# Transposes between units, and a gate projection in four parts among the levels of a two-block transformer kernel

## What is computed

```python
o_a = gated_delta_rule_chunked(q_a, k_a, v_a, beta, log_decay)   # then norm and gate z
o_b = native_sparse_attention(q_n, k_cmp, v_cmp, k_slc, v_slc, k_win, v_win, gates, ...)
merged = (sigmoid(merge_a) * (o_a @ w_branch_gdn) + sigmoid(merge_b) * (o_b @ w_branch_nsa))
x = x + merged @ w_out
gate, up = split(rms_norm(x, ffn_norm_gain) @ w_gate_up, 2)
x = x + (silu(gate) * up) @ w_down                               # then a last rms_norm
```

## Time and profile before

| | |
|---|---|
| Median of 3 runs | 912.6 us (912.44 to 913.03) |
| Profiled execution | 912.57 us, its span 910.8 us |
| Granted TensorE clock, mean | 0.997 |
| Busy: PE, DVE, ACT, POOL | 888.0, 567.8, 437.8, 52.8 us |
| DMA | 151.71 MB, mean 167 GB/s |

### The profile page before, as it was taken

One profiled execution on the slowest core, in us unless ns is written; L12 is line 12 of the kernel. 1 busy time (PEld: TensorE's weight loads), 2 busy tenths in 40 slices (PEclk: granted clock), 3 DMA queues, 4 the chain that ended last, 5 costly groups with the idle time before them and its releaser, 6 DMA issues.

```text
span 910.8 us, 14487 instructions
## 1 busy us (share of the span) xinstructions
PE 888.0 (97%) x5984; PEld 776.8 (85%) x5984; DVE 567.8 (62%) x856; ACT 437.8 (48%) x632; POOL 52.8 (6%) x79
## 2 busy tenths in 40 slices
PE   7999999999999999999999999999999999999997
PEld 5999999899999888888779999677877788888885
DVE  4955564573657665655569878754376677777544
ACT  6744444744344544444356514753434455555441
POOL 1000000000030110000020141000000000000000
PEclk9999999999999999999999999999999999999999
DMA  9657744455455545555667665004664565655441
GB/s 297 222 185 216 225 140 138 139 185 184 125 156 184 184 145 180 164 195 188 215 188 160 166 138 188 1 3 139 139 231 151 171 188 188 187 186 193 170 162 46
DMA packets 127799, 151.71 MB, mean 167 GB/s; under 512 B 16967, under 2 KB 93126, under 8 KB 127734
## 3 DMA queue, kind: packets, MB, share of 16 engines
q1 hardware_dynamic: 127594, 150.70, 53.3%
q0 software_dynamic: 64, 0.07, 0.0%
q10 hardware_dynamic: 76, 0.02, 0.0%
HBM read 148.67 MB, written 3.68 MB: 167 GB/s over the span
## 4 chain that ended last, share of the span: by engine, by line
PE 88%; DVE 6%; ACT 2%; DMA 1%; issue 1%; SPq 1%; POOL 0%; POOLq 0%; DVEq 0%; ACTq 0%
PE bank L511 21%; PE bank L513 20%; PE bank L512 20%; PE bank L1217 9%; PE bank L1205 5%; DVE w_lo L1907 2%; DVE arena L2268 1%; DMA arena<-in_mem 1%; PE bank L790 1%; PE bank L915 1%; PE bank L691 1%; PE bank L671 1%; PE bank L1029 1%; PE bank L1010 1%; ACT w_hi L1393 1%
## 5 line engine op out<-in xcount | busy, mean ns | idle before, releaser
L1907 DVE TENSOR_TENSOR w_lo<-ring,w_hi 128x2048 fp32r<-128x2048 f32 (+1 forms) x134 | 301.0, 2251 | 176.3 <-ACT w_hi L1393 175.8
L1393 ACT ACTIVATE w_hi<-ring 128x2048 fp32r<-128x2048 f32 (+1 forms) x134 | 250.2, 1870 | 124.0 <-PE bank L513 83.4
L511 PE MATMUL bank<-h_both,w_hi 128*128 128x256 f32 x624 | 179.3, 287 | 1.7 <-DVE w_lo L1907 1.7
L512 PE MATMUL bank<-h_both,w_hi 128*128 128x256 f32 x624 | 176.5, 283 | 0.0
L513 PE MATMUL bank<-h_both,w_lo 128*128 128x256 f32 x624 | 176.5, 283 | 0.0
L1217 PE MATMUL bank<-h_both,w_hi 128*128 128x512 f32 x352 | 123.4, 398 | 0.0
L511 PEld LDWEIGHTS bank<-h_both,w_hi 128*128 128x128 f32 x624 | 119.6, 192 | 3.8 <-DVE w_lo L1907 2.3
L512 PEld LDWEIGHTS bank<-h_both,w_hi 128*128 128x128 f32 x624 | 119.7, 192 | 0.6 <-issue 0.5
L513 PEld LDWEIGHTS bank<-h_both,w_lo 128*128 128x128 f32 x624 | 119.7, 192 | 0.0
L1205 PE MATMUL bank<-h_both,w_lo 128*128 128x256 f32 x352 | 97.8, 281 | 0.4 <-ACT h_both L1416 0.4
L1408 ACT ACTIVATE arena<-bank 128x512 f32<-128x512 f32 (+5 forms) x91 | 45.5, 522 | 100.3 <-PE bank L513 87.3
(11 more groups left out here) (332 smaller groups left out, 1362.4 us busy)
## 6 DMA issues: line engine op xcount, KB each, us to landing
ring<-in_w_in SPq DMA_DIRECT2D x59, 1024.0 KB, 5.2
ring<-in_w_gate_up SPq DMA_DIRECT2D x44, 512.0 KB, 4.6
ring<-in_w_down SPq DMA_DIRECT2D x10, 1024.0 KB, 5.0
ring<-in_w_mem_kv SPq DMA_DIRECT2D x8, 1024.0 KB, 7.1
ring<-in_w_in SPq DMA_DIRECT2D x8, 512.0 KB, 4.9
ring<-in_w_gla_out SPq DMA_DIRECT2D x4, 1024.0 KB, 5.0
ring<-in_w_x_out SPq DMA_DIRECT2D x4, 1024.0 KB, 5.1
ring<-in_w_dsa_out SPq DMA_DIRECT2D x4, 1024.0 KB, 5.7
```

Of the source, the lines that this page charges most:

```text
L511: mm(o, ah, bh, start=start, stop=False, skip_group_check=True)
L512: mm(o, ah, bl, start=False, stop=False, skip_group_check=True)
L1393: act(w_hi[:, k % NHI, 0:m], ring[:, order.index(name) % NSLOT, 0:m], ACT.Copy)\
L1907: tt_(w_lo[:, i, 0:m], ring[:, i, 0:m], w_hi[:, k % NHI, 0:m].bitcast(F), ALU.subtract)\
```

## The change

Six edits. The identity is loaded from ACT's queue, ahead of its parameters. A new `rows_projection` opens all four banks and orders a projection as unit 0a, the last transposes, 1a, 0b, 1b, for both `wo` and `w2o`. The compressed transposes and their copies move into step 3; the output of step 3 waits for cp3 only before its last products. Of ma0 both units are taken at its first quarter; the four quarters (token tile, half of the channels) stand behind level 2, behind its end, and before and after step 7, with ACT's tanh of ma00 before step 3 and of ma01 after step 7; ma1, mb0 and mb1 then alternate with the GDN steps and `gdn_out` comes last. `held_units` makes names done in between count one unit less. The transposes gt stand inside bn1, T20 and T21 inside bg1; DVE's sums are ordered accordingly. The last quarter of the result is scaled and sent by ACT.

```diff
@@ -471,9 +471,11 @@
+            held_units = [0]
             def done(name, ins):
                 ins.then_inc(full(name)[0], 1)
-                splits_by[name] = len(splits)
+                splits_by[name] = len(splits) - held_units[0]
@@ -553,7 +555,7 @@
-            def tokens_part(title, unit_name, x, k0, k1, last, tag=None, pair_ready=None):
+            def tokens_part(title, unit_name, x, k0, k1, last, tag=None, pair_ready=None, between=None):
@@ -571,6 +573,19 @@
                         part_done(unit_name, ins)
+                    if between is not None and t == 0:
+                        between()
+            def rows_projection(name, x, tag, last_rows):
+                for c in range(2):
+                    for t in range(TT):
+                        open_bank(f"{name}{c}{t}")
+                tokens_part(f"{name}0", f"{name}0a", x, 0, 4, KT - 1, tag)
+                last_rows()
+                tokens_part(f"{name}1", f"{name}1a", x, 0, 4, KT - 1)
+                tokens_part(f"{name}0", f"{name}0b", x, 4, 8, KT - 1, tag)
+                tokens_part(f"{name}1", f"{name}1b", x, 4, 8, KT - 1)
@@ -842,12 +857,7 @@
-            def rest_of_rows():
-                transpose_wide("1", merged, (2, 3))
-                pe.wait_ge(*read("T13"))
-            wide_tokens("wo0", (mg_hi, mg_lo), rest_of_rows, tag="1")
-            wide_tokens("wo1", (mg_hi, mg_lo))
+            rows_projection("wo", (mg_hi, mg_lo), "1", lambda: transpose_wide("1", merged, (2, 3)))
@@ -1029,6 +1039,8 @@
                                skip_group_check=True)
+                if r == 0:
+                    pe.wait_ge(*read("cp3"))
                 for g in range(2):
@@ -1093,8 +1105,32 @@
                     nsa_logits((i + 3) // 2)
+                if i == 3:
+                    compressed_transposes()
                 if i % 4 == 3:
                     nsa_out(i // 4)
+            gate_parts = []
+            def first_gate(t, half):
+                if not gate_parts:
+                    gate_parts.extend([split_unit("ma0a", 512), split_unit("ma0b", 512)])
+                    held_units[0] = 1
+                wh, wl = gate_parts[half]
+                if half == 0:
+                    open_bank(f"ma0{t}")
+                s, k0 = slice(128 * t, 128 * t + 128), 4 * half
+                for k in range(k0, k0 + 4):
+                    ins = three(bank_of(f"ma0{t}")[:, :], (h_hi[:, k, s], h_lo[:, k, s]), (wh[:, k - k0, :], wl[:, k - k0, :]),
+                                k == 0, k == KT - 1)
+                if half == 1:
+                    done(f"ma0{t}", ins)
+                if (t, half) == (1, 0):
+                    part_done("ma0a", ins)
+                    held_units[0] = 0
+                if (t, half) == (1, 1):
+                    unit_used["ma0b"] = full("ma01")
@@ -1106,17 +1142,20 @@
             level(2)
+            first_gate(0, 0)
             nsa_step(1)
...
             level_end(2)
-            compressed_transposes()
+            first_gate(0, 1)
             nsa_step(3)
...
             nsa_step(6)
+            first_gate(1, 0)
             nsa_step(7)
+            first_gate(1, 1)
             level(4)
@@ -1165,35 +1204,34 @@
             gdn_state(0)
-            wide_tokens("ma0", h_parts, lambda: gdn_chunk(1))
+            wide_tokens("ma1", h_parts, lambda: gdn_chunk(1))
             gdn_state(1)
-            wide_tokens("ma1", h_parts, lambda: gdn_chunk(2))
+            wide_tokens("mb0", h_parts, lambda: gdn_chunk(2))
             gdn_state(2)
-            wide_tokens("mb0", h_parts, lambda: gdn_chunk(3))
+            wide_tokens("mb1", h_parts, lambda: gdn_chunk(3))
             gdn_out()
-            wide_tokens("mb1", h_parts)
-            def merge_part(name, c, x, pair_ready=None):
+            def merge_part(name, c, x, pair_ready=None, between=None):
                 for t in range(TT):
                     open_bank(f"{name}{c}{t}")
-                tokens_part(f"{name}{c}", f"{name}{c}", x, 0, 4, 3, None, pair_ready)
+                tokens_part(f"{name}{c}", f"{name}{c}", x, 0, 4, 3, None, pair_ready, between)
             pe.wait_ge(*read("no3"))
+            def gdn_transposes():
+                pe.wait_ge(*read("gd1"))
+                for j in range(2):
+                    bank = open_bank(f"gt{j}")
+                    for hh in range(2):
+                        for t in range(TT):
+                            ins = nc.tensor.transpose(bank[:, 256 * hh + 128 * t:256 * hh + 128 * t + 128],
+                                                      gd_rows[:, 4 * t + 2 * j + hh, :], ident)
+                    done(f"gt{j}", ins)
             merge_part("bn", 0, (oT_hi, oT_lo))
-            merge_part("bn", 1, (oT_hi, oT_lo))
-            pe.wait_ge(*read("gd1"))
-            for j in range(2):
-                bank = open_bank(f"gt{j}")
-                for hh in range(2):
-                    for t in range(TT):
-                        ins = nc.tensor.transpose(bank[:, 256 * hh + 128 * t:256 * hh + 128 * t + 128],
-                                                  gd_rows[:, 4 * t + 2 * j + hh, :], ident)
-                done(f"gt{j}", ins)
+            merge_part("bn", 1, (oT_hi, oT_lo), None, gdn_transposes)
             merge_part("bg", 0, (z2_hi, z2_lo), "z2_split")
-            merge_part("bg", 1, (z2_hi, z2_lo))
-            transpose_wide("2", ma, range(4))
-            wide_tokens("w2o0", (m2_hi, m2_lo), tag="2")
-            wide_tokens("w2o1", (m2_hi, m2_lo))
+            merge_part("bg", 1, (z2_hi, z2_lo), None, lambda: transpose_wide("2", ma, (0, 1)))
+            rows_projection("w2o", (m2_hi, m2_lo), "2", lambda: transpose_wide("2", ma, (2, 3)))
             transpose_tokens("f", xn, 2)
@@ -1253,7 +1291,6 @@
                 sp.dma_start(xres[:, t, :], A["x"][0, 128 * t:128 * t + 128, :]).then_inc(signal(f"x_in{t}"), 16)
-            sp.dma_start(ident, consts[:, 0:128]).then_inc(signal("ident_in"), 16)
             for i, name in enumerate(order):
@@ -1322,7 +1359,7 @@
             for t in range(TT):
-                for c in range(2):
+                for c in range(2 - t):
                     sp.wait_ge(signal("result"), 2 * t + c + 1)
@@ -1357,6 +1394,7 @@
+            sc.dma_start(ident, consts[:, 0:128]).then_inc(signal("ident_in"), 16)
             at = 0
@@ -1677,9 +1715,9 @@
-            def merge_gate(name):
+            def merge_gate(name, tiles=range(TT)):
                 dst, c = (ma, mb)[name[1] == "b"], int(name[2])
-                for t in range(TT):
+                for t in tiles:
                     title = f"{name}{t}"
@@ -1700,6 +1738,8 @@
                     causal_exp("n", i + 4)
+                if i == 3:
+                    compressed_copies()
                 if i % 4 == 3:
@@ -1714,11 +1754,12 @@
             nsa_step(2)
-            compressed_copies()
+            merge_gate("ma0", (0,))
             nsa_step(3)
...
                 nsa_step(i)
+            merge_gate("ma0", (1,))
             level_copy(4)
@@ -1732,9 +1773,9 @@
             nsa_step(15)
-            merge_gate("ma0")
             merge_gate("ma1")
             merge_gate("mb0")
+            merge_gate("mb1")
             for t in range(TT):
@@ -1743,7 +1784,6 @@
             ins.then_inc(signal("sumsq_d"), 1)
-            merge_gate("mb1")
             highs(splits_by["gt1"] + 2)
@@ -1780,6 +1820,12 @@
                     half_squares("o", xres[:, t, 512 * c:512 * c + 512], 0, c, t)
+            sc.wait_ge(signal("last_product"), 1)
+            sc.wait_ge(signal("rstd_o"), 2)
+            last = xn[:, 1, 512:1024]
+            act(last, last, ACT.Copy, scale=rstd[:, 3:4]).then_inc(signal("last_result"), 1)
+            sc.wait_ge(signal("last_result"), 1)
+            sc.dma_start(out[0, 128:256, 512:1024], last).then_inc(signal("out_done"), 16)
@@ -2488,12 +2534,15 @@
                 tt_(gd_rows[:, s, :], by_head(f"gd{t}"), rb, ALU.mult).then_inc(reader(f"gd{t}"), 1)
-            for c in range(2):
-                for t in range(TT):
-                    title = f"bn{c}{t}"
-                    v = mb[:, t, 512 * c:512 * c + 512]
-                    bank_ready(title)
-                    stt(v, v, 1.0, bank_of(title)[:, :], ALU.add, ALU.mult).then_inc(reader(title), 1)
+            def nsa_branch(c, t):
+                title = f"bn{c}{t}"
+                v = mb[:, t, 512 * c:512 * c + 512]
+                bank_ready(title)
+                stt(v, v, 1.0, bank_of(title)[:, :], ALU.add, ALU.mult).then_inc(reader(title), 1)
+            nsa_branch(0, 0)
+            nsa_branch(0, 1)
+            nsa_branch(1, 0)
             for j in range(2):
@@ -2501,20 +2550,28 @@
                 tt_(pair(z2_lo, j), pair(z2, j), pair(z2_hi, j).bitcast(F), ALU.subtract).then_inc(signal("z2_split"), 1)
-            for c in range(2):
-                for t in range(TT):
-                    title = f"bg{c}{t}"
```

(36 more changed lines are left out.)

## The result

| | before | after |
|---|---|---|
| Median | 912.0 us (17 runs) | 914.6 us (17 runs) |
| Ratio to before | | 1.0027, 95% interval 1.0019 to 1.0034 |
| Profiled execution | 912.57 us, span 910.8 | 912.87 us, span 911.1 |
| Mean granted clock | 0.997 | 0.994 |

The changed kernel is slower by 0.3%, not faster by 0.1%. One thing is needed to read its times: they lie in two groups, six of 17 at 912.7 to 913.7 us (median 912.9) and the others at 914.3 us and above (median 914.9). The profile is of the first group. So there are two questions: why the first group is no faster than before, and what adds 2.0 us to most executions.

The account below looks back on a forecast made before the run. TensorE, busy 888.0 of 910.8 us, was taken as the bound, so only its waits and low clock could yield. Terms summed to -2.0 us with the clock held, +1.0 for a fall at z: 912.57 to 911.5 us, range 909.0 to 913.8.

Parts of the forecast that it names:

- Start: Kernel start: loading the identity first on ACT's queue gains 0.2 us, between a loss of 0.3 and a gain of 0.7.
- First output projection: In wo, unit 1a covers the 1.6 us wait for low parts of merged rows: gain 1.6 us, nothing else late.
- Levels: Levels and sparse attention: 3.8 us of wait and low clock go, new costs 0.8, 0.3, 1.5, 0.2: -1.0 us.
- Last products: Last products of output 0: PE waits 1.5 us for ACT's compressed copies, queued behind exponentials of steps 6 and 7.
- Islands: Four quarters among the levels are four more entries and exits of projection matmuls: 0.8 us lost (0 to 0.9).
- GDN branch: Wait for z before bg0 grows from 2.05 to 3.5 us behind DVE's splits and sums; 1.6 us lost with cut transposes.
- Clock in that wait: In the wait for z before bg0, the clock was expected to fall, costing 1.0 us (0 to 1.7).
- held clock: Rival: the clock holds in the wait for z before bg0, giving 910.6 us; chance 0.25.
- Second merge: Second merge and output projection: the 0.8 us wait at the last transposes goes, islands cost 0.1: gain 0.7 us.
- End: Kernel end: ACT scales and sends the last result quarter, gain 0.1 us, from a loss of 0.2 to a gain of 0.3.
- paced by ACT and DVE: Rival: splits delay the softmax in the levels, compressed wait 3.75 us with low clock, 915.5 us; chance 0.10.
- Both waits let the clock fall: Rival: clock falls both at the compressed copies and at z, at the lengths forecast, 913.2 us; chance 0.10.

Follow-up runs that it names:

- high_first: Changed kernel with ScalarE taking the second gate-up unit's high part ahead of the squares of the second output projection: 913.1 us, ratio 1.0009.
- ends_back: Changed kernel with the identity back on SyncE's queue and the last result quarter back on VectorE and SyncE: 914.6 us, one run.
- again: Changed kernel run once more with no edit: 915.1 us, ratio 1.0025 to the kernel before.
- copies_first: Changed kernel with ScalarE's four compressed copies ahead of its exponentials of step 3: 913.2 us, ratio 1.0013.
- fill_six: Changed kernel with four identity products instead of two before the transposes of f, six instead of four before y: 914.1 us, ratio 1.0021.
- z_fill: Changed kernel with three identity products put into TensorE's wait for z, ahead of bg0: 913.0 us, ratio 1.0012.
- five_fixes: Changed kernel, quarters kept, with z products, gate-up high part and compressed copies moved earlier, six identity products at y, old end: 908.4 us, ratio 0.9960.
- all_fixes_gate_back: Changed kernel without quarters in the levels; z products, gate-up high part, compressed copies earlier; six identity products at y; old end: 906.6 us, ratio 0.9941.
- before_fill: Kernel before with two identity products in its 2.1 us wait ahead of the compressed transposes: 911.2 us, ratio 0.9997.

## Why the prediction was right or wrong

**Start**, -0.2 us: -0.38 us in the profile (24.90 to 24.52), less than the spread between profiles. Open.

**First output projection**, -1.6 us: the step "nothing else is late" failed. Identity products of y come 1.84 us earlier than the start explains, and the wait behind them grows from 1.32 to 2.03 us. What was gained there is -1.1 us.

**Levels**, -1.0 us: the terms, in order. The 2.1 us wait and the low clock went, as said. Bank of ma00 0.36 us (said 0.3). Last products 1.31 us, released by ACT (said 1.5). Islands 0.47 us and the third and fourth quarter 0.49 us, mostly in output 1 (said 0.8 and 0.2; the 0.2 does not follow from the 1.9 us against 1.4 + 0.9 us that it is given for). ACT split ma1a at 568.86, behind four copies, as said. Sum -2.09 + 0.49 + 0.47 = -1.1 us. Right. But the wait at the last products was taken as the price of the move; it was the price of an order on ScalarE that nothing asked for.

**GDN branch**, +1.6 us: from the start of the GDN output (649.76 and 658.18) to bg0 it is 28.77 us before, less 11.01 for mb1 17.76, and 18.85 after: +1.1 us, a wait of 2.99 us where 3.5 us was said. Right in mechanism and in what stands ahead of the z products.

**Clock in that wait**: here is the first failure of size. I forecast the fall, with the held clock as a rival (0.25). Both outcomes are common: in the seven profiles with this wait the clock held in three (after, high_first, ends_back) and fell in four. Where it fell it cost 1.6 (again, copies_first) to 2.7 us (fill_six), not 1.0: very little of the low stretch lies in the wait itself.

**Second merge**, -0.7 us: bg0 to the identity products of f is 35.61 us before, 35.01 after: -0.6 us. Right.

**What had no term**: the transposes of f. From the identity products to the last matmul it is 189.57 us before and 191.47 after: **+1.9 us**, 1.1 of it wait and 0.8 low clock (z_fill, with the wait and a held clock, has 6.61 us up to gate-up; high_first has 5.56). The prediction reordered w2o and stopped at its last matmul. It followed each unit's split to the unit that needs it, but not to the sums queued behind it, though the same rule had just been used for z. This is the step that failed most: with it the sum with the clock held is -0.1 us.

**End**, -0.1 us: +0.5 us. ScalarE's own time for the scaling (0.72 us) was left out, and with it there is no gain on VectorE's row. But the loss is not the end edit's: five_fixes and all_fixes_gate_back have it with the old end. It goes with the queue of the identity, the edit priced under **Start**, for which the prediction looked at the start alone. The Trainium skill (DMA: Bandwidth & Descriptors, "Issuing engines are not separate DMA queues") was weighed rightly as a rule against a gain: 7.5 to 7.6 us with the new end and with the old one.

**Rivals.** None is the right one. By the number, 915.5 us is nearest to the 914.6 us measured, but that would be luck: the stretch was not paced by ACT and DVE (1.3 us of wait at the last products, not 3.8). "Both waits let the clock fall", 913.2 us, had the right kind of loss, at z and, in one profile (ends_back), behind the last products too. In all: -2.1 us to f, +1.9 behind it, +0.5 at the end, and in eleven of 17 executions some 2 us, 1.6 of them in the profile of again for the clock at z. The start of the sum adds to it: 912.57 us is 0.6 us above the median of the kernel before, 912.0 us, and the 1.7 us of low clock at the transposes that it takes off was perhaps not lost in every execution of the kernel before (before_fill).

## What to carry to other kernels

When a projection's units are reordered, follow the splits of the *next* units too: they sit in the vector engines' queues between the sums that the following norm needs. When a wait has been explained, look at what the releasing engine was itself waiting for; two lines moved on ScalarE (copies ahead of exponentials) were worth as much as the quarters of a whole gate (levels 2 to 3 in 11.03 us without quarters, 17.53 - 5.74 = 11.79 us with them and the old order). And a wait that moves to a place after a dense stretch is to be priced with both outcomes of the clock, from rows that have each. Where one run puts back two edits, as ends_back does, look through the other runs for one that has only one of them before the cost is put down to either.
